# Gated recurrence: scores woven with output products, output chunks parted by linear blocks

## The reference

```
q, f, i, g = split(h @ w_in)                 # four linear blocks of 128 columns a head
fg = lb + (1-lb)*sigmoid(f); k = 1-fg; v = i; q = silu(q)
G = cumsum(log fg) within a chunk
A[t,s] = sum_k q[t,k] k[s,k] exp(G[t]-G[s]), s <= t          # the scores of a chunk
o = A v + (q*exp(G)) S ;  S = exp(G_last) S + (k*exp(G_last-G))^T v
x += (rms_norm(o) * silu(g)) @ w_out         # the output product of the head
```

## Time and profile before

| | before |
|---|---|
| median of three runs | 3793.66 us |
| the profiled execution's own time | 3798.4 us |
| its span | 3796.8 us |
| TensorE busy | 3537.1 us (93%) |
| VectorE busy | 2125.4 us (56%) |
| ScalarE busy | 1170.7 us (31%) |
| mean granted TensorE clock | 0.92 of full |

### The profile page before, as it was taken

The page is one execution under the profiler, slowest core; times in us unless marked ns, Lnnn a source line. Parts: engine busy times, 40 slices in busy tenths (PEclk is TensorE's granted clock), DMA queues, the critical chain, the costliest instruction groups (busy, mean ns, idle before and its releaser), DMA issues. The chain is left out here.

```text
span 3796.8 us, 55091 instructions
## 1 busy us (share of the span) xinstructions
PE 3537.1 (93%) x19764; PEld 3151.5 (83%) x19780; DVE 2125.4 (56%) x3935; ACT 1170.7 (31%) x1961; POOL 224.8 (6%) x349
## 2 busy tenths in 40 slices
PE   5999999998999999999978995899989999999997
PEld 4988889886899999999853692454579999999996
DVE  5465555654655545555678776763333555455556
ACT  4222333321411111111335866674433111111112
POOL 3000000000100000000100001100002000000001
PEclk8888888887999999999957996999999999999998
DMA  2110011100111111111201121012431111111111
GB/s 90 35 40 29 29 40 35 40 29 23 36 45 45 40 40 45 45 40 42 88 12 56 74 78 41 12 37 111 177 129 36 48 37 40 45 51 35 40 45 64
DMA packets 57414, 192.33 MB, mean 51 GB/s; under 512 B 7016, under 2 KB 23408, under 8 KB 52528
## 3 DMA queue, kind: packets, MB, share of 16 engines
q1 hardware_dynamic: 52992, 167.89, 12.8%
q0 software_dynamic: 4144, 20.71, 1.5%
HBM read 166.64 MB, written 21.93 MB: 50 GB/s over the span
## 5 line engine op out<-in xcount | busy, mean ns | idle before, releaser
L292 PE MATMUL ff1lin<-ff1h_hi,ff1w_hi 128*128 128x384 f32 x1056 | 354.9, 336 | 10.3 <-DVE ff1w_lo L286 5.7
L292 PE MATMUL ff0lin<-ff0h_hi,ff0w_hi 128*128 128x384 f32 x1056 | 354.1, 335 | 7.3 <-DVE ff0w_lo L286 4.4
L293 PE MATMUL ff1lin<-ff1h_lo,ff1w_hi 128*128 128x384 f32 x1056 | 353.8, 335 | 0.0
L294 PE MATMUL ff1lin<-ff1h_hi,ff1w_lo 128*128 128x384 f32 x1056 | 353.8, 335 | 0.0
L293 PE MATMUL ff0lin<-ff0h_lo,ff0w_hi 128*128 128x384 f32 x1056 | 353.3, 335 | 0.0
L294 PE MATMUL ff0lin<-ff0h_hi,ff0w_lo 128*128 128x384 f32 x1056 | 353.3, 335 | 0.0
L292 PE MATMUL hg_lin<-hg_h_hi,hg_w_hi 128*128 128x384 f32 x768 | 269.6, 351 | 17.3 <-POOL hg_h_lo L165 15.4
L293 PE MATMUL hg_lin<-hg_h_lo,hg_w_hi 128*128 128x384 f32 x768 | 264.4, 344 | 0.0
L294 PE MATMUL hg_lin<-hg_h_hi,hg_w_lo 128*128 128x384 f32 x768 | 263.6, 343 | 0.0
L292 PEld LDWEIGHTS ff1lin<-ff1h_hi,ff1w_hi 128*128 128x128 f32 x1056 | 199.0, 188 | 13.1 <-DVE ff1w_lo L286 6.3
L292 PEld LDWEIGHTS ff0lin<-ff0h_hi,ff0w_hi 128*128 128x128 f32 x1056 | 198.7, 188 | 8.6 <-DVE ff0w_lo L286 4.7
(11 more groups left out here) (429 smaller groups left out, 7807.0 us busy)
## 6 DMA issues: line engine op xcount, KB each, us to landing
ff_raw<-in_weights SPq DMA_DIRECT2D x132, 512.0 KB, 3.3
hg_raw<-in_weights SPq DMA_DIRECT2D x40, 512.0 KB, 3.3
as_keys<-in_cache_k SPq DMA_DIRECT2D x16, 1024.0 KB, 4.8
as_vals<-in_cache_v SPq DMA_DIRECT2D x8, 2048.0 KB, 9.9
se_keys<-in_cache_ki SPq DMA_DIRECT2D x8, 1024.0 KB, 4.8
pb_raw<-in_weights SPq DMA_DIRECT2D x12, 512.0 KB, 3.3
x<-in_x SPq DMA_DIRECT2D x3, 1536.0 KB, 8.7
x_keep<-x POOLq DMA_DIRECT2D x1, 4608.0 KB, 17.4
```

Source lines behind the costliest of these rows:

```text
L292: pe.matmul(out, w_hi, x_hi, start=start, stop=False)
L293: pe.matmul(out, w_hi, x_lo, start=False, stop=False)
L294: return pe.matmul(out, w_lo, x_hi, start=False, stop=stop)
```

## The change

On TensorE steps 2 and 3 are woven: two chunks of scores (16 small matmul records each), then two units of the output product, eight times; after that the streams' scores (734), then the last 8 units. Step 6 and 7 are woven: the first block of v stands behind output chunk 5, the second behind chunk 11, and the third behind the streams' outputs. The two waits ahead of the first output unit now stand behind the first two chunks of scores. Bodies without an output product (1) keep the old order of step 2, and body 8, without blocks of v, that of step 6.

On VectorE the order becomes: `v_own`, additions 0 to 5, low part of the f slab, additions 6 to 15, the masks, additions 16 to 23, the chain of states, low part of the v slab, new states of the streams.

```
 (VectorE)
                 r = h - 1
-                if has(h, 1, 9):
+                def mask_scores():
                     hold(dve, att_done, r + 1, tk)
...
+                def add_out(n):
+                    nb, g = divmod(n, G)
+                    hold(dve, W.units, units_before(h) + n + 1, tk)
+                    xs = x[:, nb, g * GT:(g + 1) * GT]
+                    dve.tensor_tensor(xs, xs, lin[g][:, 0:GT], ALU.add).then_inc(dve_evac, 1)
+
+                out_here = has(h, 2, 10)
+                if has(h, 1, 9):
                     hold(dve, ss_out, r * 16, tk)
                     dve.tensor_tensor(v_own[:, :, :], ...).then_inc(v_spread, 1)
+                if out_here:
+                    dve.drain()
+                    for n in range(6):
+                        add_out(n)
                 if has(h, 0, 8) and body_slabs(h):
                     lo(h, par0, 0)
...
+                if out_here:
+                    for n in range(6, NC):
+                        add_out(n)
+                if has(h, 1, 9):
+                    mask_scores()
+                if out_here:
+                    for n in range(NC, KB * G):
+                        add_out(n)
...
+                if has(h, 0, 8):
+                    lo(h, par0, 1)
+                if has(h, 1, 9):
                     hold(dve, ds_done, r * 3 + 3, tk)
...
                 if has(h, 0, 8):
-                    lo(h, par0, 1)
 (TensorE)
+                def attend(c):
...
+                def out_unit(n):
+                    nb, g = divmod(n, G)
+                    if n == 0:
+                        hold(pe, n_dve, (h - 2) * 2 + 2, tk)
+                        hold(pe, W.lo_done, slab_base(h) + 1, tk)
+                    if n < G and has(h, 2, 9):
+                        hold(pe, act_evac, h * 12 - 2 + n, tk)
+                    else:
+                        hold(pe, dve_evac, (h - 2) * 24 + n - 2, tk)
+                    W.product(pe, lin[g][:, 0:GT], par0, nb * P, ...).then_inc(W.units, 1)
+
+                out_here = has_out and has(h, 2, 10)
+                for c in range(0, NC, 2):
+                    if has(h, 1, 9):
+                        attend(c)
+                        attend(c + 1)
+                    if out_here:
+                        out_unit(c)
+                        out_unit(c + 1)
+                if has(h, 1, 9):
                     pe.matmul(rb[4][:, 0:P], k_mids[:, :], ...).then_inc(att_done, 1)
...
+                if out_here:
+                    for n in range(NC, KB * G):
+                        out_unit(n)
...
+                def values_block(g):
+                    if g == 0:
+                        hold(pe, W.lo_done, slab_no(h, 1) + 1, tk)
+                    hold(pe, act_evac, h * 12 + g + 1, tk)
+                    W.block(pe, lin[g][:, 0:GT], pars(par0, h, 1), h_hi, h_lo, g).then_inc(W.units, 1)
+
+                for c in range(NC):
+                    if has(h, 1, 9):
                         rows = slice(c % 2 * CH, (c % 2 + 1) * CH)
...
+                    if has(h, 0, 8) and c in (5, 11):
+                        values_block(c // 6)
...
                 if has(h, 0, 8):
-                    hold(pe, W.lo_done, slab_no(h, 1) + 1, tk)
-                    for g in range(G):
-                        hold(pe, act_evac, h * 12 + g + 1, tk)
-                        W.block(pe, lin[g][:, 0:GT], pars(par0, h, 1), h_hi, h_lo, g).then_inc(W.units, 1)
+                    values_block(2)
```

More of the change, by code:

```diff
@@ L612, in body @@
                     W.split_lo(dve, 39, 1, 1)
-                if has(h, 2, 10):
-                    dve.drain()
-                    for nb in range(KB):
-                        for g in range(G):
-                            hold(dve, W.units, units_before(h) + nb * G + g + 1, tk)
-                            xs = x[:, nb, g * GT:(g + 1) * GT]
-                            dve.tensor_tensor(xs, xs, lin[g][:, 0:GT], ALU.add).then_inc(dve_evac, 1)
+                if out_here:
[6 more added lines that the diff above has]
+                        add_out(n)
                 if has(h, 1, 9):
@@ L726, in body @@
                     i.then_inc(turned, 1)
[L727 to L733, removed]
@@ L734, in body @@
-                    pe.matmul(rb[4][:, 0:P], k_mids[:, :], q_mid[:, T_PROMPT:T], start=True, stop=True).then_inc(att_done, 1)
[L735 to L747, removed]
+                def attend(c):
+                    rows, col = c % 2 * CH, c // 2 * CH
+                    for i_ in range(NS):
+                        n = SB * (i_ + 1)
+                        at = k_at(i_) + c * n
+                        pe.matmul(rb[3][rows:rows + n, col + i_ * SB:col + (i_ + 1) * SB], k_mid[:, at:at + n],
+                                  q_mid[:, c * CH + i_ * SB:c * CH + (i_ + 1) * SB], start=True, stop=True)
@@ new lines, in out_unit @@
+                def out_unit(n):
[7 more added lines that the diff above has]
+                        hold(pe, dve_evac, (h - 2) * 24 + n - 2, tk)
+                    W.product(pe, lin[g][:, 0:GT], par0, nb * P, o_hi[:, g * GT:(g + 1) * GT],
+                              o_lo[:, g * GT:(g + 1) * GT], True, True).then_inc(W.units, 1)
@@ L772, in body @@
                               start=True, stop=True).then_inc(ds_done, 1)
-                    for c in range(NC):
+                def values_block(g):
[5 more added lines that the diff above has]
+                    if has(h, 1, 9):
                         rows = slice(c % 2 * CH, (c % 2 + 1) * CH)
```

## The result

The changed kernel takes 3755.18 us (median of four runs, 3738.97 to 3757.98), the kernel before 3792.49 us in the runs beside it (3790.45 to 3795.4). The ratio is 0.9886, with a 95% interval of 0.9871 to 0.99: faster by 1.1%, inside the range, 14 us above the forecast of 3741. The profiled execution took 3757.98 us, span 3756.4, so against 3798.4 it is 40.4 us shorter where I had 53.

The account below looks back on a forecast made before the run. TensorE, busy 93% of the span, was taken as the bound, partly at half clock and stalled by VectorE. Savings of 35 + 18 = 53 us from 3793.7 gave 3741 us, range 3708 to 3775 us.

Parts of the forecast that it names:

- Stretch A: Transposes to state increments, lines 725 to 753: 25.4 us against 30.46, saving 35 us over seven bodies.
- The stall: TensorE's wait for a VectorE addition, ahead of output unit 3: would move to unit 19, shrinking from 2.86 to 1.7 us.
- changes of kind: Switches between small and large matmuls, 15 in the weave: 0.1 us each, 1.5 us (0 to 6).
- I expect it to stay up: TensorE's clock in the weave of scores and output units: no fall, a condition of saving 5.0 us a body.
- the sign of being wrong: In the weave of scores and output units: a clock under 0.9 would show the forecast wrong.
- rival 3: Clock falls in the weave: Stretch A 39 us, 8.5 us over today, kernel slower at 3836 us; chance 0.07.
- the 0.56: Share of weaves with a fallen clock from which the kernel would end slower than before.
- Stretch B: Output chunks and blocks of v, lines 771 to 793: 2.6 us saved a body from 34.40, 18 us (0 to 37).
- the streams' outputs at the low clock: In Stretch B, the 16 records of the streams were priced at 3.4 us.
- the falls went where I said: In Stretch B, clock falls after runs of small matmuls would lie mostly over dense blocks, losing 1.6 us each.
- What was to be hidden: VectorE's key decays after `o_done`: would end at 33 us, ScalarE needing them at 35.8, cover 3 us; priced at nothing.
- The rule that I weighed: Skill's rule for TensorE's clock: avoid idle gaps over about 3 us; as only condition, weaving busy work moves no clock.

Follow-up runs that it names:

- before_unrolled: The kernel before the change, with the ten bodies of TensorE and VectorE written out instead of looped; 3781.52 us, ratio 0.9961.
- unit_first: The changed kernel with each pair of output units placed ahead of its two chunks of scores; 3770.81 us, ratio 0.9943.
- weave_only: The changed kernel with the three blocks of v, and VectorE's low part of their slab, put back behind `o_done`; 3768.88 us, ratio 0.9939.
- fine: The changed kernel, loops kept, with v's blocks split into single products behind each output chunk, every second streams' product, and `o_done`; 3714.69 us, ratio 0.9799.
- adds_first_fine: The changed kernel, loops kept, with v's blocks split into single products and v spread for the streams only after additions 0 to 5; 3719.29 us, ratio 0.9809.

## Why the prediction was right, and where it was off

- **Stretch A, at full clock, was right.** 25.65 us against the 25.4 of the sum. The stall moved to unit 19 and is 1.50 us (forecast 1.7). Scores and sixteen units took 328.19 - 309.91 = 18.28 us; the parts without changes of kind are 16.4, so one costs 0.12 us (I had taken 0.1).
- **The step that failed is "I expect it to stay up".** It did in five of seven bodies; in bodies 4 and 6 the clock was 0.58, under the 0.9 that I had named as the sign of being wrong. I had leaned on the 26 us of dense blocks ahead of the weave and had not looked at what stands between them and it. The fallen weaves are rival 3 in two places: 36.63 and 36.81 us where I had priced 39. Five good bodies save 23.2 us, two fallen ones lose 11.5. Had all stood at 25.6, A would have given 34 us of the 35. The share of fallen weaves, 2/7 = 0.29, lies below the 0.56 at which this rival would have made the kernel slower.
- **The trace of before had the sign.** The pauses stand there too, ahead of bodies 4 and 6:

```profile
433.36 1.18 PE L725 MATMUL hg_rec<-c_ident,hg_k_end 128*128 128x128 f32 x9 [1.11 <-issue]
...
651.67 1.17 PE L725 MATMUL hg_rec<-c_ident,hg_k_end 128*128 128x128 f32 x9 [1.00 <-issue]
```

The scores of these two bodies held 1.00 for 2.95 us and 3.08 us, those of the five others for 3.93 to 5.65 us; in `before_unrolled`, without the pauses, all seven held it for 4.1 to 5.1 us. So the 2.95 us that I read as small matmuls alone, with TensorE never idle, was a run behind an idle time. The 2.89 us of the output chunks of body 3 has none ahead of it.
- **Why they fell.** Shown: idle time of about a microsecond at the entry of the weave can bring the fall (none of seven without it, three of seven with it, same code otherwise), and the back edges of TensorE's and VectorE's loops make such idle time in bodies 4 and 6. The profiled executions of all kernels that weave scores first say the same: of 46 weaves without such idle time none fell, of 17 with some 1.0 to 1.6 us of it eight did. The trend is the same in `unit_first`, where a wait of 0.81 us stood in the weave; that this wait brought down body 7 there is argued, not shown.
- **Stretch B was mis-sized, the other way.** 3.9 us a body against 2.6. I had the streams' outputs at the low clock, 3.4 us, and in five bodies of seven they ran in 1.86; the falls went where I said, mostly onto the blocks, with 6.8 to 13.7 us at the low clock a body. 27 us in place of 18.
- **The sum.** 35 - 22 (two falls, 2 x 11.1) - 1 (weaves 0.2 us longer than the sum) + 9 (B) = 21 + 18 = 39 us, against 53: the 40.4 of the profiled executions. That the median came within 14 us of the forecast is in part luck: A gave 23 us less than I had said and B 9 us more.
- **What was to be hidden was.** `k_end` and `k_mid`: VectorE's key decays started when `o_done` came and ended before ScalarE turned to them, as the two lines of the changed kernel show; 378.7 is their end (three smaller groups follow the one shown), 5.5 us ahead, where I had 3.

```profile
374.17 3.03 DVE L674 TENSOR_TENSOR hg_k_mid<-hg_G 128x256 f32<-128x256 f32 x4 [4.14 <-PE hg_rec L821]
...
384.19 2.35 ACT L538 ACTIVATE hg_k_mid<-hg_k_mid 128x2560 f32<-128x2560 f32 x1
```

- **The rule that I weighed.** To avoid idle gaps of more than about 3 us between bursts (the Trainium skill, "TensorE: Matmul & The Clock Gate", "Why this matters for your kernels") is not enough here. Falls came with TensorE busy throughout (body 5 of before), and the idle times at the entry of fallen weaves were 0.8 to 1.6 us. The trace disagrees with it as the only condition, as it did before.

**Open.** What decides between a weave that stands and one that falls behind the same pause. The added pause brought down three of seven, all with the same entry; `weave_only` lost body 4, behind 1.57 us, and not body 6, behind 1.32; `fine` and `adds_first_fine` lost none of their four in the executions with a profile, behind 1.03 to 1.48 us. So the length of the pause does not settle it. Whether it is where the pause falls in time, by whatever the chip goes by when it sets the clock, was not tried. The spread of the changed kernel's runs, 3738.97 to 3757.98, is what a weave or two more that stand would give at 11 us each, and `fine`'s one run of 3723.66 what one fall would give; those runs have no trace. Why `fine` keeps its weaves, whose entry it does not touch, was not settled either.

## What to carry to other kernels

Small matmuls should stand between dense ones in pieces as short as the data allow, one product at a time and not a block at a time, as far as any other engine's waits allow: a busy TensorE is no sign that it is fast. Where such a weave follows a wait or a loop's back edge, fill or remove the idle time at its entry, on every engine that the weave waits for in its first microseconds. And read the granted clock body by body: a mean would have shown a gain of 1.7 us a body here, and not five bodies that gained 4.6 and two that lost 5.8.

## What the runs showed of the hardware

- The back edge of an instruction loop cost TensorE 1.33 and 1.48 us and VectorE 1.82 us in the rows above, each put down to "issue", once every two bodies (TensorE 1.00 to 1.57 us over all kernels with loops). Written out, the engine had no such pause.
- A mix of about half small and half dense matmuls kept the clock at 2.4 GHz where it was up and no idle time stood at the entry (25.65 us), and at 1.2 GHz where it was down (30.68 us in one piece, with TensorE never idle).
- The streams' outputs, eight accumulating matmuls of 16 columns in sixteen records, take 1.86 us at the high clock and 3.43 at the low one, which is in line with the clock and not with a fixed cost of an instruction.
- VectorE's additions took 0.517 us each in the written-out kernel and 0.54 in the loop, with the same operands. In body 8 of the kernel before, which stands behind the loop, 19 took 9.93 us, 0.523 each. Why was not tried.
